# Padded decode reads, earlier fed products and a split scatter wait in a two-layer recurrent decoder step

## The reference

```python
def step(S, inp):                       # one chunk of 64 tokens; q, k decayed by the gates
    o = scores @ vb + q_dec @ S         # outputs of the prompt
    S = S * s_dec + k_dec.T @ vb
    return S, o
# a decode token b is a chunk of one: S_b = S_b * exp(g_b) + k_b^T v_b ;  o_b = q_b S_b
o = rms_norm(o, norm_w) * silu(g)       # layer 0 heads and layer 1; the groups add d_skip * x first
for e in range(N_EXPERTS):
    y = y + gates[:, e:e+1] * ((silu(t @ w_gate[e]) * (t @ w_up[e])) @ w_down[e])
```

## Time and profile before

| what | value |
|---|---|
| median of 3 runs | 1032.12 us |
| the profiled execution | 1031.38 us, span 1029.7 us |
| mean granted clock of PE | 0.986 |
| PE busy | 977.8 us (95%) |
| DVE, ACT, POOL busy | 388.3, 277.0, 107.9 us |
| layer 0: heads, groups, out-projection | about 66 to 160, 160 to 237, 237 to 305 us |
| layer 0 experts | 318 to 552 us |
| layer 1: projection, heads | 565 to 605, 605 to 733 us |
| layer 1 experts | 779 to 1012 us |

### The profile page before, as it was taken

One profiled execution on the slowest core, in us unless ns is written; L12 is line 12 of the kernel. 1 busy time (PEld: TensorE's weight loads), 2 busy tenths in 40 slices (PEclk: granted clock), 3 DMA queues, 4 the chain that ended last, 5 costly groups with the idle time before them and its releaser, 6 DMA issues.

```text
span 1029.7 us, 12780 instructions
## 1 busy us (share of the span) xinstructions
PE 977.8 (95%) x5031; PEld 631.6 (61%) x5031; DVE 388.3 (38%) x936; ACT 277.0 (27%) x591; POOL 107.9 (10%) x177
## 2 busy tenths in 40 slices
PE   8999999899989999999997998999989999999995
PEld 6777777688866454545444876777866354545443
DVE  2467786773025021212113335665235021212114
ACT  4534434223023110000002166777123100100002
POOL 2322224161000000000000001112200000000000
PEclk9999999899998999999999999999999999999999
DMA  9933536947751999999999343332692999999991
GB/s 386 356 156 123 210 138 229 394 178 297 285 194 33 424 411 424 421 420 422 422 422 427 145 164 121 138 130 87 254 374 89 423 413 423 420 422 421 422 378 44
DMA packets 39183, 299.65 MB, mean 291 GB/s; under 512 B 5000, under 2 KB 6536, under 8 KB 8648
## 3 DMA queue, kind: packets, MB, share of 16 engines
q1 hardware_dynamic: 33696, 268.52, 64.1%
q0 software_dynamic: 4928, 29.72, 7.8%
q10 hardware_dynamic: 496, 0.53, 0.1%
HBM read 283.32 MB, written 15.53 MB: 290 GB/s over the span
## 4 chain that ended last, share of the span: by engine, by line
PE 76%; ACT 8%; DVE 7%; DMA 6%; issue 2%; POOL 1%; ACTq 0%; DVEq 0%; POOLq 0%
PE bank L1182 20%; PE bank L1206 10%; PE bank L827 9%; PE bank L1076 6%; PE bank L1218 5%; PE bank L1167 5%; PE bank L1330 4%; PE bank L1096 2%; PE bank L1343 2%; DMA ring<-in_w_up 2%; ACT ring L1515 2%; PE bank L1110 1%; PE bank L1104 1%; DMA spread<-v_rows 1%; DMA W<-in_conv_cols 1%
## 5 line engine op out<-in xcount | busy, mean ns | idle before, releaser
L1182 PE MATMUL bank<-ring,A 128*64 128x512 f32 x880 | 223.0, 592 | 2.3 <-issue 1.7
L827 PE MATMUL bank<-xT,ring 128*128 128x264 f32 x704 | 165.0, 390 | 2.7 <-ACT A L1428 1.4
L827 PEld LDWEIGHTS bank<-xT,ring 128*128 128x128 f32 x704 | 132.0, 191 | 32.7 <-issue 9.3
L1182 PEld LDWEIGHTS bank<-ring,A 128*64 128x64 f32 x880 | 73.8, 137 | 123.9 <-issue 123.9
L1206 PE MATMUL bank<-ring,W 128*64 128x512 f32 x448 | 113.4, 595 | 0.9 <-ACT W L1658 0.9
L2223 DVE TENSOR_TENSOR W<-W,bank 128x512 f32<-128x512 f32 x16 | 11.0, 688 | 203.6 <-PE bank L1182 203.6
L1343 PE MATMUL bank<-xT,ring 128*128 128x264 f32 x320 | 80.0, 395 | 0.0
L1206 PEld LDWEIGHTS bank<-ring,W 128*64 128x64 f32 x448 | 34.9, 137 | 60.9 <-issue 59.8
L754 POOL TENSOR_SCALAR xT<-xT,vecs 128x264 f32<-128x264 f32 x4 | 5.6, 1396 | 604.3 <-DVE xT L2077 604.3
L1343 PEld LDWEIGHTS bank<-xT,ring 128*128 128x128 f32 x320 | 58.4, 192 | 11.0 <-issue 1.8
L1218 PE MATMUL bank<-W,A 128*128 128x264 f32 x256 | 63.5, 392 | 1.7 <-issue 1.7
(11 more groups left out here) (310 smaller groups left out, 1180.5 us busy)
## 6 DMA issues: line engine op xcount, KB each, us to landing
ring<-in_w_gate SPq DMA_DIRECT2D x56, 1024.0 KB, 13.2
ring<-in_w_down SPq DMA_DIRECT2D x56, 1024.0 KB, 13.4
ring<-in_w_up SPq DMA_DIRECT2D x54, 1024.0 KB, 16.2
ring<-in_w_ab SPq DMA_DIRECT2D x10, 2048.0 KB, 8.2
ring<-in_w_c SPq DMA_DIRECT2D x8, 2048.0 KB, 13.7
A<-in_w_up SPq DMA_DIRECT2D x10, 1024.0 KB, 13.9
ring<-in_w_oab SPq DMA_DIRECT2D x4, 2048.0 KB, 9.2
A<-in_w_gate SPq DMA_DIRECT2D x8, 1024.0 KB, 12.8
```

What stands on the lines that cost most here:

```text
L827: mm = pe.matmul(ab_bank(m)[:, 0:T], slot(AB_IN0 + m // 4, 8)[:, c, (m % 4) * P:(m % 4 + 1) * P], xT[:, c, :], start=(c == 0), stop=(c == ...
L1182: mm = pe.matmul(bank[i][64 * j:64 * j + 64, :], xg[:, 2 * (pair % 2) + j, c, :], slot(n0 + 6 * pair + 2 * i + j, 8)[:, c, :], start=(c == ...
```

## The change

It has five parts. (1) Reads are padded: the stationary side of a read is 32 columns of which one holds the query and the others zero (column 0 for i = 0, column 1 for i = 1), and the two halves accumulate in one range, so that read b stands alone in row 32q + i. Squares, sums, roots and scaling then cover half as many read columns, and the turn is one ordinary transpose for each 128 columns, into a bank of its own (6, or 2 and 4 for the last head of a layer) instead of the score bank; DVE places one copy for each 128 columns. The zeros are written once per layer by POOL, for the groups by DVE, which also copies C's decode columns into their places. In the groups both reads stand ahead of the four fed products and are copied once. A wait moves from `scores` to `turn_v`, one is new in `turn_out` (for ACT's copy of the decode rows, which shares bank 6), one new ahead of `out_part(1)`. (2) `C_FEED`: two of the products of layer 1 stand ahead of turn_out instead of behind it. (3) In layer 1 ACT does `copy_v(0)` ahead of the exponentials of head 1. (4) `scatter` waits for the copy of its own half only. (5) `spread_eg(0)` (two transfers of POOL's queue) moves from the end of the heads to behind `spread_x(0)`, since its target shares columns with the padded queries.

```diff
-C_FEED = (2, 2, 1, 2, 2, 1, 2, 2, 0, 2, 2, 2)
+C_FEED = (2, 4, 1, 0, 2, 1, 2, 2, 0, 2, 2, 2)
...
+        def query_columns(h):
+            at = 5632 + 256 * (h % 2)
+            return W[:, at:at + 258].rearrange("p (i x) -> p i x", x=129)[:, :, 0:P:32]
+        def padded_query(h, b):
+            at = 5632 + 256 * (h % 2) + 32 * b
+            return W[:, at:at + 32]
-        def read_turned(layer, J):
-            return bank[4][:, 256:256 + J * NB] if layer else bank[2][:, 400:400 + J * NB]
+        def read_turned(n, J):
+            return bank[{3: 2, 11: 4}.get(n, 6)][:, 256:256 + J * P]
...
+            st.add(pool.memset(W[:, 5632:6144], 0.0))
...
-            spread_eg(0)
             pool.wait_ge(sem("heads_out_ready"), 3)
...
             spread_x(0)
+            spread_eg(0)
             store_states(0, GLA_ST0, gla_s)
...
+                    if h >= 3:
+                        pe.wait_ge(sem("heads_reads_placed"), n - 2)
...
-                    if h >= 2:
-                        pe.wait_ge(sem("heads_reads_placed"), n - 1)
...
-                            mm = pe.matmul(bank[3][32 * q:32 * q + 32, i * dv:(i + 1) * dv],
-                                           QS[:, h % 2, b:b + 1].to_broadcast([P, 32]), decode_state(layer, h, b),
-                                           start=True, stop=True)
+                            mm = pe.matmul(bank[3][32 * q:32 * q + 32, 0:dv],
+                                           padded_query(h, b), decode_state(layer, h, b),
+                                           start=(i == 0), stop=(i == 1))
...
                     pe.wait_ge(sem("heads_scaled"), n + 1)
-                    for i in range(NB // 4):
-                        for j in range(J):
-                            mm = pe.matmul(read_turned(layer, J)[:, j * NB + 4 * i:j * NB + 4 * i + 4],
-                                           READ[:, i * dv + j * P:i * dv + (j + 1) * P], every32, start=True, stop=True)
-                    mm.then_inc(sem("heads_reads_turned"), 1)
+                    pe.wait_ge(sem("heads_kv_copied"), 3 * min(n + 2, H0 + nh - 1) + 2)
+                    for j in range(J):
+                        tr = pe.transpose(read_turned(H0 + h, J)[:, j * P:(j + 1) * P], READ[:, j * P:(j + 1) * P], ident[:, :])
+                    tr.then_inc(sem("heads_reads_turned"), 1)
...
                 reads(0)
+                reads(1)
                 feed(4)
                 pe.wait_ge(sem("ssd_prompt_state"), g + 1)
-                reads(1)
-                for i in range(2):
-                    pe.wait_ge(sem("ssd_reads_copied"), 2 * g + i + 1)
-                    for j in range(4):
-                        mm = pe.matmul(bank[4][:, 256 + j * NB + 4 * i:260 + j * NB + 4 * i],
-                                       s_read[:, i, j * P:(j + 1) * P], every32, start=True, stop=True)
-                mm.then_inc(sem("ssd_state_used"), 1)
+                pe.wait_ge(sem("ssd_reads_copied"), g + 1)
+                for j in range(4):
+                    tr = pe.transpose(bank[7][:, j * P:(j + 1) * P], s_read[:, j * P:(j + 1) * P], ident[:, :])
+                tr.then_inc(sem("ssd_state_used"), 1)
...
             out_part(0, gla_half)
+            pe.wait_ge(sem("ssd_outputs_read"), 3)
             out_part(1, gla_half)
...
                 def scatter(pair, p, half):
 
-                    for i in range(2):
-                        pe.wait_ge(sem(f"y_copied{i}"), p + 2)
+                    pe.wait_ge(sem(f"y_copied{half}"), p + 2)
...
-                    act.activation(READ[:, 0:2 * dv], bank[3][:, 0:2 * dv], ACT.Square, scale=dv ** -0.5).then_inc(
+                    act.activation(READ[:, 0:dv], bank[3][:, 0:dv], ACT.Square, scale=dv ** -0.5).then_inc(
...
+                if layer == 1:
+                    copy_v(0)
                 exps(layer, 1)
                 st.run(act.activation(decx[:, 0:nh, :], (gkg[:, 0:4, NP:T] if layer == 0 else A[:, 8:16, NP:T]), ACT.Exp))
-                copy_v(0)
+                if layer == 0:
+                    copy_v(0)
...
-                for i in range(2):
-                    act.wait_ge(sem("ssd_reads_ready"), 2 * g + i + 1)
-                    act.copy(s_read[:, i, :], bank[5 + 2 * i][:, :]).then_inc(sem("ssd_reads_copied"), 1)
-                    if i == 0:
-                        take_ab(m0 + 5)
+                act.wait_ge(sem("ssd_reads_ready"), g + 1)
+                act.copy(s_read[:, :], bank[5][:, :]).then_inc(sem("ssd_reads_copied"), 1)
+                take_ab(m0 + 5)
...
-                    for i in range(2):
-                        st.add(dve.tensor_scalar(READ[:, i * dv:(i + 1) * dv], bank[3][:, i * dv:(i + 1) * dv],
-                                                 hms[:, h % 2, 2 + i:3 + i], None, ALU.mult))
+                    st.add(dve.tensor_scalar(READ[:, 0:dv], bank[3][:, 0:dv], hms[:, h % 2, 2:3], None, ALU.mult))
...
+                if g == 0:
+                    st.run(dve.memset(s_cz, 0.0))
+                dve.wait_ge(sem("conv_silu"), CONV.index(C0 + g) + 1)
+                st.add(dve.tensor_copy(s_cz_columns, A[:, C0 + g, NP:T].rearrange("p (i q) -> p i q", i=2)))
```

More of the change, by code:

```diff
@@ L763, in _ @@
             stage_end(pool, 4)
-            st.run(pool.memset(SC_BLOCKS, 0.0))
+            st.add(pool.memset(SC_BLOCKS, 0.0))
+            st.add(pool.memset(W[:, 5632:6144], 0.0))
+            st.settle()
             pool.sem_inc(sem("scores_cleared"), 1)
@@ L1888, in sums @@
                         dve.wait_ge(sem("heads_squared"), 2 * n + i + 1)
[L1889 to L1890 removed]
+                        red = dve.tensor_reduce(hms[:, h % 2, 2 * i:2 * i + 2 - i],
+                                                squares[:, 0:(2 - i) * dv].rearrange("p (i v) -> p i v", v=dv), AX, ALU.add)
                         st.add(red)
```

36 lines of the change are left out of this document (19 added, 17 removed).

## The result

The changed kernel took 1022.1 us (median of 4, 1017.3 to 1022.8) beside 1032.1 for the kernel before: a ratio of 0.987, 95% interval 0.984 to 0.991. Repeated on another chip it was 1022.5, and 55 executions of the kernel before had a median of 1034.1. So the change is worth 10 to 12 us, where 20.3 were summed; 1022 lies outside the range of 1007 to 1019.

What follows compares the result with a forecast made beforehand. The chain was taken as 76% TensorE (PE), with layer 1's heads nearly as much ScalarE's. Terms 1.6 + 2.8 + 0 + 1.7 + 4.9 + 6.3 + 3.0 = 20.3 us off 1031.38, with median and miss allowances, gave 1012; range 1007 to 1019.

Steps and rivals of the forecast that it cites:

- Layer 0's heads: Turns of layer 0's heads: two transposes replace eight instructions, 0.53 us saved in three of four; 1.6 us, bounds 1.3 to 1.8.
- State-space groups: Two state-space groups: four transposes replace 16 instructions in turning the reads, 1.4 us saved in each; 2.8, bounds 2.3 to 3.1.
- rival B: Layer 0's experts: weight stream does not move with PE, so 4.4 us gained before it are lost; 1016; chance 0.07.
- The clock: Between the state-space groups: half-speed stretch of about 3.3 us stays, so gain counted 0; other end 1.6 us.
- A half clock at a place that had none: Anywhere in the trace: one of the signs listed as showing the forecast wrong; no size given.
- Scatter by halves: End of each layer's experts: PE's 0.84 us wait before the last scatter goes; 1.7 us in all, bounds 1.2 to 1.7.
- Start of layer 1's heads: Layer 1's first decode rows leave 3.1 us earlier; 4.5 plus 0.4 for shorter squares and scaling, 4.9 us, bounds 2.0 to 5.8.
- Rival A: Layer 1's heads: a turn stays near 13.9 us, giving 2.5 instead of 6.3; 1016 to 1018; chance 0.17.
- Turns: Five turns of layer 1's heads: each falls from 14.41 to 13.15 us, PE's floor 13.0; 6.3 us, bounds 2.5 to 7.5.
- rival D: New wait for ACT's copy of the decode rows holds PE in eleven turns; slower, over 1035; chance 0.03.
- rival C: Clock does not fall between the groups (1.6 us) and layer 1's start or turns reach their far bound; 1007 to 1009; chance 0.18.
- Last two turns: Last two turns of layer 1's heads: 0.7 and 1.8 us saved, last L930 0.5; sum 3.0, bounds 2.0 to 3.3.

Runs made afterwards that it cites:

- part 3: Scatter's old waits restored in the changed kernel, 1021.3 us (before 1032.5); scatter by halves alone in the kernel before, 1036.5 (1032.5); two further runs, 1021.4 and 1014.1 (1035.5).

## Why the prediction missed

**Layer 0's heads**, 1.6 summed. The table load at their end stood at 158.92 to 159.21 in four profiles of kernels with the old heads and at 156.52 to 158.00 in eleven with the new, 157.37 on the mean: 1.7. (A twelfth, the run with the old wait at one place, has 159.81 and a half clock at 72.0 to 75.4.) Right. That after's own profile shows 3.9 in this stretch is luck: the kernel before had a half clock from 161.4 to 164.8, which ten of the sixteen profiles don't have, after's among them.

**State-space groups**, 2.8 summed, -2.5 measured. This is the failed step. As PE work the term was right, since with the fills held L1033/L1047 to the output projection shrinks by 5.7, of which the two half clocks of the kernel before with the hold (the first products 3.29 instead of 1.97, and 1.7 between the groups) make 3.0 and the work 2.6. But I had priced `out_part(1)`, POOL's issues and DVE's copies, and never asked who brings the second group's operands, and when. The first two w_oab fills leave once the heads' states are stored (188 to 193 in the eleven profiles), and the third as soon as PE has read the buffer that it overwrites. In the changed kernel the DMA engines stay about 0.9 or more busy till 216, and the rows land at 218. A faster PE here even brings the third fill forward, to 204.9 to 207.3 in eight profiles from 208.7 to 212.1 in three, against the very rows that PE waits for next. Of this shape was rival B ("if that stream did not move with PE"), but I had put it at the experts' weights. One profile without a wait there had looked like slack; in the two other profiles of old kernels there was a wait already.

**The clock.** I counted 0 between the groups, with 1.6 as the other end; the end came true. In none of the twelve profiles with turned reads is there a half clock at 194 to 206, in two of four with the old reads there is. The transposes of the next group and the idle time of 0.87 us ahead of them are there in both. For the changed kernel the window reads:

```profile
194.00:196.00 2.00, 1.13 (x10) 1.00 0.99 410
196.00:198.00 2.00, 2.00 (x18) 1.00 1.00 360
```

The Trainium skill ("TensorE: Matmul & The Clock Gate", Part 4: PE-mode transpose) says that transposes do not count as work for the clock. This case doesn't bear out what I drew from it: four transposes, 0.87 us of nothing and fourteen more small instructions passed at full clock. Elsewhere the clock cost something that I had put at nothing, and this is the second term that failed. "A half clock at a place that had none" stood among the signs against me, and it came, behind layer 0's experts, 5.9 us in the profiled execution. The eight unfilled profiles of part 3 put this place at 4.4. Over whole executions the net cost is smaller, since half clocks went elsewhere: the mean granted clock was 0.9845 in eight of after and 0.986 in 55 of before. A straight line through the 55 gives 6.3 us for each 0.01 (before's extremes: 1027.7 at 0.989, 1040.8 at 0.980), so the mean difference is about 1 us. The spread itself makes one execution a poor witness for a term of 2 us.

**Scatter by halves**, 1.7 summed. The 0.84 went at both places in the trace, so the wait was read rightly. In time the kernel before gained nothing by it (1.003), and the changed kernel's pair doesn't resolve it. In every profile with this edit the half clock of the paragraph above stands behind it, and I had no term for that.

**Start of layer 1's heads**, 4.9 summed, 3.4 came. I had named the cause ("less if the spread has to share with the whole fill") and took 4.5 for its part; it measured 2.2 with the edit undone, and 3.0 from before's trace to after's. The update began at 622.56, not near 616. The low half of my bounds was the better choice, since the fill that had slowed the store was only to meet the spread instead. Rival A's path was not needed.

**Turns**, 6.3 summed, 6.5 came, with PE's floor (13.0) and the paths as worked out. Rival A (the turn keeps its length) falls, and so does rival D: PE waited 0.2 us before L944. Of rival C the clock stayed up between the groups, as it says, but the time that this was to bring didn't come. In turn_v PE waited 2.1 us for the states, 1.3 of it at the start.

**Last two turns**, 3.0 summed, 2.1 plus 0.3 for the last one's own length.

So of 20.3 us the edits gave some 17 where the transfers let them. One slip in the range: 1007 is called the middle of C, which is 1008; it decides nothing. The range failed because it treated the shift of the groups as certain: with the fills as they are, what is gained ahead of the second group's update is lost to a DMA, 4 to 6 us that no rival held, and because it had no term for a half clock at a new place. The first is shown by the held fills, which bring the kernel to 1014.2, inside the range, while the same hold gives the kernel before 3.1. The cause of the second stays open.

## What to carry to other kernels

Ahead of every gain on the bound engine, look at the next place where that engine meets data brought by DMA, and ask whether the transfer starts sooner too and what it then runs beside. Here a transfer of 16 KB issued beside fills of 2 MB each took 9.45 us instead of 1.8, and holding the fills back by one wait on their queue gave 8 us, more than the largest edit. Ask also which fills the faster engine itself sets free earlier. Where the clock varies from one execution to the next, read a term of 1 or 2 us from several traces, as distances between marks, and not from one.

## What the runs showed of the hardware

The second group's store of 16 KB took 1.8 us with the fills held back (the DMA engines at most 0.05 busy) and 3.6 to 9.5 in the eleven profiles without the hold (0.4 to 1.0 busy), in each of them landing just behind the transfers ahead of it in its queue. The spread of 512 KB took 3.6 us with the fill held and 8.4 beside it. PE stood idle for 3.45 and 4.40 us where its program has a branch and the trace shows no other engine that it waits for. The clock's low stretches of the same program differ in place and number between executions: the kernel after had one at 222.1 to 229.0 in the one profile and at 226.0 to 229.5 in the other, and the first alone had none at 161.
